# A hybrid delta-rule and sparse-attention block on one core: the triangular inverse turned once per level, and the attention mask moved from TensorE to VectorE

## What is computed

```python
# branch A: gated delta rule, 8 heads, (the kernel works in chunks of 128 tokens)
a_mat = jnp.where(strict, jnp.einsum('bhnid,bhnjd->bhnij', kb, k) * gamma, 0.0)
sol = lax.linalg.triangular_solve(a_mat + eye, rhs, left_side=True, lower=True)
...
v_new = u_n - w_n @ S ; o = qg_n @ S + attn_n @ v_new ; S = S * exp(dl) + kd_n^T @ v_new
oa = rms_norm(oa, gdn_norm_g) * jax.nn.silu(za)          # "gating" below
# branch B: attention of 8 heads over the 256 best keys of each token
logits = einsum('bqhc,bqkc->bqhk', ql, kv) + bias
logits = jnp.where(valid, logits, -jnp.inf)              # here a mask of 0 and -1e30
p = jax.nn.softmax(logits, axis=-1); o = einsum('bqhk,bqkc->bqhc', p, kv)
```

## Time and profile before

| | |
|---|---|
| median of 3 runs | 1651.97 us (1646.09 to 1652.5) |
| the profiled execution, its own time | 1650.57 us |
| its span, first to last instruction | 1648.7 us |
| front, to the delta phase's first DMA | 505.7 us |
| delta phase, from there to attention's first DMA | 1254.1 us |
| attention, from there to the merge's first DMA | 1467.6 us |
| merge | the rest |
| mean granted TensorE clock | 0.98 of full speed |
| busy: PE, DVE, ACT, POOL | 93%, 62%, 32%, 31% of the span |

### The profile page before, as it was taken

How to read it: one execution, slowest core, us unless ns; L and a number is a source line. 1 busy time by engine, 2 the same in 40 slices (tenths; PEclk the granted TensorE clock), 3 DMA queues, 4 the chain that set the end, 5 groups by cost and what they waited for, 6 DMA issues and landing times. The chain is left out here.

```text
span 1648.7 us, 27285 instructions
## 1 busy us (share of the span) xinstructions
PE 1541.3 (93%) x10038; PEld 957.1 (58%) x10038; DVE 1019.9 (62%) x1873; ACT 526.8 (32%) x1181; POOL 506.1 (31%) x543
## 2 busy tenths in 40 slices
PE   2899999999998999989898899999997999999997
PEld 2455884444444567757676676654443778864443
DVE  6629999999992455555555655434522666638333
ACT  2428321111112433543534334232101565531111
POOL 2420122222223543441431414123423333356000
PEclk9999999999999999999999999999998999999999
DMA  9100223323212222121210202236463000036122
GB/s 375 57 31 22 71 81 123 102 96 102 89 65 79 55 64 54 27 66 32 61 54 26 66 20 73 90 90 217 157 228 116 14 27 14 27 138 215 56 101 77
DMA packets 130876, 142.69 MB, mean 87 GB/s; under 512 B 17194, under 2 KB 104530, under 8 KB 128980
## 3 DMA queue, kind: packets, MB, share of 16 engines
q1 hardware_dynamic: 118676, 120.31, 23.2%
q10 hardware_dynamic: 12096, 20.98, 3.5%
HBM read 110.18 MB, written 31.08 MB: 86 GB/s over the span
## 5 line engine op out<-in xcount | busy, mean ns | idle before, releaser
L92 PE MATMUL ps<-g_h_hi,g_piece_hi 128*128 128x512 f16 x544 | 211.0, 388 | 4.3 <-PEq L1957 4.3
L93 PE MATMUL ps<-g_h_lo,g_piece_hi 128*128 128x512 f16 x544 | 210.0, 386 | 0.0
L94 PE MATMUL ps<-g_h_hi,g_piece_lo 128*128 128x512 f16 x544 | 209.7, 385 | 0.0
L92 PE MATMUL ps<-g_h_hi,a_w_hi 128*128 128x512 f16 x448 | 171.1, 382 | 6.9 <-DVE g_h_lo L523 5.2
L93 PE MATMUL ps<-g_h_lo,a_w_hi 128*128 128x512 f16 x448 | 171.1, 382 | 0.0
L94 PE MATMUL ps<-g_h_hi,a_w_lo 128*128 128x512 f16 x448 | 170.9, 382 | 0.0
L613 DVE MATCH_REPLACE8 a_ada<-a_best,a_ada 128x1024 f32<-128x1024 f32 (+2 forms) x192 | 166.6, 875 | 0.0
L610 DVE MAX8 a_best<-a_ada 128x8 f32<-128x1024 f32 (+2 forms) x192 | 160.9, 880 | 0.7 <-DVE a_ada L599 0.3
L837 POOL CAST g_piece_hi<-g_piece 128x1024 f16<-128x1024 f32 x41 | 47.9, 1169 | 343.8 <-PE ps L94 204.7
L239 POOL CAST a_w_hi<-a_w 128x2048 f16<-128x2048 f32 x14 | 26.5, 1891 | 273.8 <-PE ps L94 273.8
L1066 DVE SCALAR_TENSOR_TENSOR g_yq<-e_raw,g_taps,g_yq 128x1024 f32<-128x1024 f32 x60 | 90.7, 1512 | 28.6 <-ACT g_yq L913 26.5
(11 more groups left out here) (316 smaller groups left out, 3623.7 us busy)
## 6 DMA issues: line engine op xcount, KB each, us to landing
a_w<-in_w_in SPq DMA_DIRECT2D x18, 1024.0 KB, 5.7
g_piece<-in_w_in SPq DMA_DIRECT2D x34, 512.0 KB, 4.3
channel_gates<-a_x ACTq DMA_DIRECT2D x48, 256.0 KB, 2.0
e_lb<-diagonal_blocks SPq DMA_DIRECT2D x32, 256.0 KB
a_ada<-in_w_ada ACTq DMA_DIRECT2D x4, 1024.0 KB, 10.6
a_ada<-in_w_ada SPq DMA_DIRECT2D x4, 1024.0 KB, 15.8
a_x<-in_x SPq DMA_DIRECT2D x8, 512.0 KB, 20.8
delta_gate<-a_x ACTq DMA_DIRECT2D x32, 128.0 KB, 1.8
```

The costliest lines, as they stand in the source:

```text
L92: pe.matmul(out, a_hi, b_hi, start=first, stop=False)
L93: pe.matmul(out, a_hi, b_lo, start=False, stop=False)
L94: return pe.matmul(out, a_lo, b_hi, start=False, stop=last)
```

## The change

Four things change.

1. The inverse: `turn_base` now runs at each of the levels (u = 28, 34 and 40), and ACT copies `b1` each time. The product sets that updated `b1` (L1379, L1393) and their subtractions go. The steps of levels 16 and 32 move up by two to four slots: `expand` from u = 31 to 27, `middle16` and `x16` from 34 to 30, `outer16` 36 to 32, `middle32` and `x32` 38 to 36, `outer32` and its subtraction 40 to 38.
2. `x32` becomes the same memory as `x16`. DVE zeroes the blocks in between again at u = 46, and `gate_load` loses its wait for `tx64` and moves from slot 20 to slot 3, to the place right after the gating of the head before.
3. The mask: the identity product goes, and `peak` becomes one fused operation that adds the mask to the logits, writes the negated sum to `p`, and takes the minimum. The exponential reads `p` instead of PSUM, and the logits of step n wait for the peak of step n - 2 instead of its exponential.
4. The order of tiles within a head is (0, 7, 1, 6, 2, 5, 3, 4) instead of (7, 0, 6, 1, 5, 2, 4, 3).

```diff
-        x32 = zb[:]
+        x32 = x16
...
-                sp.wait_ge(tx64, min(h + 3, H))
...
-                if slot % SLOTS == 20 and 0 <= (slot - 92) // SLOTS < H:
+                if slot % SLOTS == 3 and 0 <= (slot - 75) // SLOTS < H:
...
# ACT
-                    if u == 38:
+                    if u == 36:
                         act.wait_ge(xm32, h + 1)
+                        act.wait_ge(tx16, h + 1)
...
-                    if u == 32:
-                        act.wait_ge(bt, h + 1)
+                    if u in (28, 34, 40):
+                        act.wait_ge(bt, 3 * h + (u - 28) // 6 + 1)
...
# DVE
-                    if u == 40:
+                    if u == 38:
                         dve.wait_ge(tx32, h + 1)
...
-                            nc.vector.tensor_tensor(b1[odd, :, even], b1[odd, :, even], short(3)[odd, :, cols], ALU.subtract).then_inc(up32, 1)
...
-                    if u == 36:
+                    if u == 32:
                         dve.wait_ge(tx16, h + 1)
-                        nc.vector.tensor_tensor(blocks(b1, 16, 0), blocks(b1, 16, 0), short(3).rearrange("p i (c w) -> p i c w", w=16),
...
+                    if u == 46:
+                        dve.wait_ge(tx64, h + 1)
+                        dve.wait_ge(x64_ok, h + 1)
+                        nc.vector.memset(blocks(x16, 16, 1), 0.0).then_inc(pad, 1)
...
-                    if u == 31:
+                    if u == 27:
                         expand(h)
...
# PE
-            def turn_base(h):
-                pe.wait_ge(b2_ok, h + 1)
-                if h:
-                    pe.wait_ge(t_ok, h)
+            def turn_base(h, level):
+                if level == 0:
+                    pe.wait_ge(b2_ok, h + 1)
+                    if h:
+                        pe.wait_ge(t_ok, h)
+                elif level == 1:
+                    pe.wait_ge(up16, h + 1)
+                else:
+                    pe.wait_ge(up32, 2 * h + 2)
                 for i in range(NT):
                     last = nc.tensor.transpose(at(2, i), t2[:, h % 3, i], ident)
...
-                for i in range(NT):
-                    mm(half_at(3, i), t2[:, h % 3, i], columns(x16[:, i], 16, 0), start=True, stop=True)
...
-                for i in range(NT):
-                    mm(half_at(3, i), t2[:, h % 3, i], columns(x32[:, i], 32, 0), start=True, stop=True)
...
-                    if u == 32:
-                        turn_base(h)
+                    if u in (28, 34, 40):
+                        turn_base(h, (u - 28) // 6)
...
-ORDER = (7, 0, 6, 1, 5, 2, 4, 3)
+ORDER = (0, 7, 1, 6, 2, 5, 3, 4)
...
-                    pe.wait_ge(exp_ok, n - 1)
+                    pe.wait_ge(top_ok, n - 1)
...
-                    last = mm(out, ident_b[:], mask[:, g.first[i] + c0:g.first[i] + c1], start=False, stop=True)
...
-                nc.scalar.activation(p[:, n % 3, 0:wide[n]], g.ps[:, at:at + wide[n]], ACT.Exp,
+                nc.scalar.activation(p[:, n % 3, 0:wide[n]], p[:, n % 3, 0:wide[n]], ACT.Exp, scale=-1.0,
...
-                nc.vector.tensor_reduce(top[:, n % 4:n % 4 + 1], g.ps[:, at:at + wide[n]], AX.X, ALU.max, negate=True).then_inc(top_ok, 1)
+                if n >= 3:
+                    dve.wait_ge(turned, n - 2)
+                at, c0 = scores_at(n), g.first[steps[n][1]]
+                nc.vector.tensor_tensor_reduce(out=p[:, n % 3, 0:wide[n]], in0=g.ps[:, at:at + wide[n]], in1=mask[:, c0:c0 + wide[n]], scale=-1.0,
+                                               scalar=-TAKEN, op0=ALU.add, op1=ALU.min, accum_out=top[:, n % 4:n % 4 + 1]).then_inc(top_ok, 1)
```

More of the change, by code:

```diff
@@ L773, in _ @@
             for slot in range(END):
-                if slot % SLOTS == 20 and 0 <= (slot - 92) // SLOTS < H:
-                    gate_load((slot - 92) // SLOTS)
+                if slot % SLOTS == 3 and 0 <= (slot - 75) // SLOTS < H:
+                    gate_load((slot - 75) // SLOTS)
                 if slot % 8 == 4 and slot // 8 + 3 < PIECES:
@@ L1370, in middle16 @@
             def middle16(h):
-                pe.wait_ge(b1_ok, h + 1)
+                pe.wait_ge(b1_ok, 3 * h + 1)
                 for i in range(NT):
@@ L1378, in outer16 @@
                 for i in range(NT):
-                    mm(half_at(3, i), t2[:, h % 3, i], columns(x16[:, i], 16, 0), start=True, stop=True)
-                for i in range(NT):
-                    last = mm(half_at(2, i), x16[:, i], columns(t2[:, h % 3, i], 16, 1), start=True, stop=True)
+                    last = mm(half_at(3, i), x16[:, i], columns(t2[:, h % 3, i], 16, 1), start=True, stop=True)
                 last.then_inc(tx16, 1)
             def middle32(h):
-                pe.wait_ge(up16, 2 * h + 2)
+                pe.wait_ge(b1_ok, 3 * h + 2)
                 for i in range(NT):
@@ L1392, in outer32 @@
                 for i in range(NT):
-                    mm(half_at(3, i), t2[:, h % 3, i], columns(x32[:, i], 32, 0), start=True, stop=True)
-                for i in range(NT):
-                    last = mm(half_at(2, i), x32[:, i], columns(t2[:, h % 3, i], 32, 1), start=True, stop=True)
+                    last = mm(half_at(3, i), x32[:, i], columns(t2[:, h % 3, i], 32, 1), start=True, stop=True)
                 last.then_inc(tx32, 1)
             def middle64(h):
-                pe.wait_ge(up32, 4 * h + 4)
+                pe.wait_ge(b1_ok, 3 * h + 3)
                 for i in range(NT):
@@ L1768, in logits @@
                     out = g.ps[:, at + c0:at + c1]
-                    three(nc.tensor, out, q_hi[:, h, tok], q_lo[:, h, tok], k_hi[:, h % 2, c0:c1], k_lo[:, h % 2, c0:c1], True, False)
                     n0, n1 = max(c0, (i - 1) * P, 0), min(c1, (i + 1) * P)
-                    if n0 < n1:
+                    near = n0 < n1
+                    last = three(nc.tensor, out, q_hi[:, h, tok], q_lo[:, h, tok], k_hi[:, h % 2, c0:c1], k_lo[:, h % 2, c0:c1], True, not near)
+                    if near:
                         b0 = n0 - (i - 1) * P
-                        for part in (bias_hi, bias_lo):
-                            mm(g.ps[:, at + n0:at + n1], flip_h[:], part[:, h, b0:b0 + n1 - n0], start=False, stop=False)
-                    last = mm(out, ident_b[:], mask[:, g.first[i] + c0:g.first[i] + c1], start=False, stop=True)
+                        mm(g.ps[:, at + n0:at + n1], flip_h[:], bias_hi[:, h, b0:b0 + n1 - n0], start=False, stop=False)
+                        last = mm(g.ps[:, at + n0:at + n1], flip_h[:], bias_lo[:, h, b0:b0 + n1 - n0], start=False, stop=True)
                 last.then_inc(logit, 1)
```

38 lines of the change are left out of this document (15 added, 23 removed).

## The result

The changed kernel takes 1628.2 us in the median of 4 runs (1624.7 to 1632.1); the kernel before, on the same chip, 1651.5 (1646.1 to 1652.5). The ratio is 0.9866, with a 95% interval of 0.9834 to 0.9898. The forecast of 1621 was 7 us too low; the time lies in its range of 1613 to 1631, near the upper end. The profiled execution took 1624.71 us and was the fastest of the four, so its phases are read beside those of the other kernels.

| us | delta | attention | merge | profiled execution |
|---|---|---|---|---|
| before | 748.4 | 213.4 | 181.2 | 1650.57 |
| after | 727.7 | 205.2 | 182.8 | 1624.71 |
| forecast for after | 732.2 | 198.9 | as before | 1619.9 |

A forecast was written before the change was run, and what follows sets the result against it. PE was taken to bound attention, and PE's work plus a DVE-POOL collision the delta phase. From the profiled 1650.57 us, -16.2 (delta) and -14.5 (attention) gave 1619.9, or 1621 for the median, range 1613 to 1631.

The forecast's parts named there:

- PE's stand in heads 0 to 2: Delta phase: PE waits for the expanded base; delays of +7.9 us in head 0, +4.6 in head 1, +1.5 in head 2.
- Heads 3 to 7: Delta phase: period 63.3 us against 69.16, so -5.9 in each of four periods and -4 in the last, -27.6 together.
- The stretch behind the last outer32: End of the delta phase: 3.5 us of products become one turn of 0.88, saving 2.65 us.
- The sum of -16.2: Whole delta phase, in us: +7.9 + 4.6 + 1.5 - 27.6 - 2.65.
- The gating wait: Delta phase, heads 3 to 7: PE's 4.73 us wait comes from DVE colliding with POOL's L864, and should go.
- The gating wait stays: Rival, delta phase: POOL and DVE still collide in slots 23 to 25; delta +2.9, kernel 1640 us; chance 0.14.
- The expansion runs into POOL: Rival, delta phase: POOL blocks DVE's expansion every time; period 64.8 plus 1.5 us, delta -3.2, kernel 1634; chance 0.08.
- the base wait in full: Rival, delta phase: waiting for the base replaces waiting for gating; periods stay at 69 us, delta +11.4, kernel 1649; chance 0.05.
- PE-bound throughout: Rival, delta phase: substitution is quicker than assumed, periods 61.3 us, kernel 1611; chance 0.10.
- the three passes: Rival, attention: the fused peak takes 2.26 us as three passes, +31 us, kernel 1667; chance 0.04.
- The forecast's -14.5: Attention: mask products removed from PE save 15.6 us, some 0.9 of it hidden at the start, +0.3 for the larger last tile.
- attention without PE idle time after its start: Expected sign in the trace after, with 182 us instead of 196 from the first to the last logits.

The follow-up runs named there:

- experiment 2: Changed kernel with the old order of tiles (7, 0, 6, 1, 5, 2, 4, 3): 1620.3 us, ratio 0.9814, attention 198.1 us.
- experiment 7: Kernel before, only POOL made to wait for an earlier head's gating before its span products and weight split: 1624.2 us, ratio 0.9833, delta phase 721.5.
- experiment 9: Changed kernel with POOL also waiting for the gating before its span products: 1625.1 us, ratio 0.9835, delta phase 733.6.
- experiment 4: Changed kernel in its new order, next head's key and value pieces moved behind the small tiles: 1620.7 us, ratio 0.9811, attention 199.2.
- experiment 3: Kernel before with only the new order of tiles: 1652.7 us in one run, attention 213.7.
- Experiment 1: Changed delta phase with the attention of the kernel before: 1632.2 us, ratio 0.9898, delta phase 730.8, attention 211.6.

## Why the prediction was right, and where it was not

**PE's stand in heads 0 to 2: right.** Forecast were waits of 9.3, 4.8 and half of that; measured 8.7, 4.7 and 2.3. Counted from the phase's first DMA, outer32 (middle32 before) comes 7.7 us later in head 0 (forecast 7.9), 4.5 more in head 1 (4.6) and 2.3 more in head 2 (1.5).

**Heads 3 to 7: right.** The four periods behind head 2 are 62.8, 63.05, 63.6 and 64.1 us, 63.4 in the mean against a forecast of 63.3, and save 24.7 us together (forecast 23.6). The last period saves 3.0 us (forecast 4), and 4.7 in the execution of experiment 2. The stretch behind the last outer32 saves 7.5 (forecast 2.65), and 4.2 in experiment 2: this term was too small. One wait of 1.53 us of L1428, at 1069.7 in the kernel before, is gone from it and was not in the sum. The clock may be another part: near the end, from 1150 to 1200, the granted clock was 0.94 before, 1.00 after and 0.97 in experiment 2. The sum of -16.2 measured -17 in the typical execution and -20.7 in the profiled one.

**The gating wait: right that POOL makes it, and shown by a run; wrong in one reading.** The collision was taken from the rows of the kernel before alone. Experiment 7 removes it with PE's work untouched and gets 27 us; experiment 9 finds nothing left to remove in the changed kernel. The text has both long stretches beside L864; the gating ran beside the split of the weight piece, which follows L864 at once (L837 and L839 above). The forecast came out even so, because the piece moves with L864. "The gating wait stays" is excluded. "The expansion runs into POOL" and "the base wait in full" are excluded by periods of 63.4 us, and so is "PE-bound throughout", which had 61.3; the fused peak's 0.83 us exclude the three passes. The expansion does lose to POOL from head 4 on in this execution: it takes 1.5, 2.4, 2.4 and 3.2 us where this rival had 3.9 every time. PE stands 0.3 to 2.0 us for it.

**Attention: the step that was mis-sized is the order, costed at nearly nothing.** The forecast's -14.5 measured -8.2. Its price for the mask products held (-13.5 to -15.3 alone), and the peak came at 0.75 + 0.08 us where 0.75 + 0.1 had been taken. The text dealt with the order in one sentence on the start, "Small tiles first also leaves less PE work ahead of that stand but ends it as much sooner". What failed is that sentence and the condition that I took for granted, "attention without PE idle time after its start". Once 2 us of PE work a head are gone, the chain from a large tile's exponentials over DVE's reciprocal and POOL's division to PE's transposes has no slack left. The new order puts the piece's subtraction in front of that reciprocal. This costs 7.1 us, shown from both sides: by the order (experiment 2) and by the pieces (experiment 4), with no such loss in the one run where the mask is on PE (experiment 3). The start's wait, 6.1 us in place of 4.8, is the smaller part. The average of busy shares that I used, DVE at 16.3 of 22.6 us, could not show it: DVE had the time, but not at that place in its order.

**The merge: 1.7 us, not forecast.** It is 182.8 us in place of 181.2, though nothing in it was changed. It is 181.2 in experiments 1 and 3 as well, and 182.7 to 182.9 in all others, experiment 7 with its attention as before among them. Windows at its start show a granted clock of 0.91 over the first 20 us in the kernel after and in experiments 1 and 7, and 1.00 before. Experiment 1 has this and still takes 181.2, so the clock at the start does not settle it. It stays open.

**The whole.** Forecast -30.7 us in the profiled execution, measured -25.9; in the medians -30.5 and -23.3. In the profiled execution the miss of 4.8 is attention +6.3, the merge +1.7 and a delta phase that began 1.5 later, less 4.5 in the delta phase. The median lies 3.5 above that execution, where 1.4 was taken, and the medians' miss is 7. That the two phases missed in opposite ways, and so hid part of each other's miss in that execution, is luck. By the experiments, the 13.6 us of PE work that the new inverse saves were paid back by PE's stand at the head of the phase, which puts outer32 of head 2 14.5 us late; the gain came from the shift that it caused.

## What to carry to other kernels

When one engine is "the bound" with a regular hole of a few us in it, look for instructions of two engines that always run side by side at the hole, and try a wait on the engine that has time to spare before taking work out: here two lines were worth 27 us. When work leaves an engine, look again at every chain with little slack that passes over the others, at the largest tile: averages of busy time don't show it, while a count of the waits by tile does. An edit that only reorders needs its own price: read what side work will fall behind which tile, on each engine in turn.

## What the runs showed of the hardware

**A short stand slows the transposes behind it.** Eight of them take 1.10 us in head 3, which has no wait, 1.97 behind 8.7 and 4.7 us, and 1.81 behind only 2.26. The windows of the kernel after (length, engines' busy times, granted clock, DMA):

```profile
562.00:564.50 2.50, 1.95 (x9) 1.86 (x10) 0.50 (x1) 0.00 (x0) 2.50 (x2) 0.50 0.00 0
...
622.00:624.50 2.50, 1.88 (x9) 1.82 (x10) 0.56 (x1) 0.00 (x0) 2.50 (x2) 0.50 0.00 0
...
683.00:685.00 2.00, 1.78 (x9) 1.69 (x10) 0.43 (x2) 0.00 (x0) 2.00 (x2) 0.61 0.00 0
685.00:688.00 3.00, 3.00 (x12) 1.08 (x10) 0.00 (x0) 2.85 (x15) 2.92 (x2) 0.69 0.00 0
747.50:749.00 1.50, 1.37 (x11) 1.12 (x11) 0.40 (x2) 0.21 (x2) 1.50 (x1) 1.00 0.05 11
```

The granted clock is 0.50 (1.2 GHz) behind the two long waits, and 1.00 (2.4 GHz) where PE had not stood. Behind the wait of 2.26 us, in which PE had done next to nothing, it is 0.61 and then 0.69, the mean of stretches at either level. Behind waits of 0.3 to 2.0 us, in heads 4 to 7, the eight take 1.09 to 1.10.

**DVE's expansion and POOL, whoever starts second.** The expansion takes 1.23 us when it starts 0.1 us ahead of POOL's span products, and these then take 2.90. Where they had started first they take 1.91, and the expansion of head 5 takes 2.41:

```profile
871.26 1.91 POOL L863 TENSOR_TENSOR e_lb<-g_const,g_g 128x1024 f32<-128x1024 f32 x1 [0.18 <-POOLq L857]
871.84 2.41 DVE L1133 TENSOR_TENSOR g_arena<-e_tc,g_const 128x1024 f32<-128x1024 f32 x1
```

It ends 1.08 us behind the end of POOL's instruction, so next to none of its 1.23 us of work was done beside it. In heads 4, 6 and 7 the distance is 1.09, 1.08 and 1.08, with 0.4, 1.3 and 2.1 us of POOL's instruction left (in head 7 it is the split of a weight piece). The Trainium skill ("SBUF — State Buffer", SBUF: two separate sides) has a VectorE instruction with two SBUF inputs blocked in full by a GpSimd instruction that reads SBUF and started first. These four rows agree with that to 0.15 us.

**The exponentials cost a little more from SBUF**: 776 ns in the mean over the same 64 tiles, in place of 746 over PSUM. Whether it costs time was not tried by itself; with the old order the steady part shows no loss from it (22.74 us a head, 1.95 less than before).
